# Where the transposes stand among the expert products of a mixture of experts

## The chip, the cores and the metric

The kernel runs on one core of one Trainium2 chip. The metric is the device time in microseconds (us) of one execution. TensorE is called PE here, its weight loads PEld, VectorE DVE, ScalarE ACT, GpSimd POOL; SyncE (SP) only issues DMAs.

## The reference

The reference is a two-layer encoder on 1024 tokens of width 1024, all in float32. Layer 0 mixes tokens by RWKV-7, layer 1 by a gated linear recurrence (HGRN2). Behind each mixer comes a mixture of experts: 32 experts with 512 inner columns, of which each token uses two. The change touches only this mixture, cut here to its core:

```python
def moe_ffn(u, w_rg, b_rg, w_re, b_re, w_in, w_out):
    # top-1 group of 4, then top-2 of its 8 experts: expert, gate
    ...
    def expert_block(args):
        xb, e = args                      # up to 128 rows of one expert
        hgu = xb @ w_in[e]                # 1024 -> 2 * 512
        return (jax.nn.silu(hgu[:, :MOE_FF]) * hgu[:, MOE_FF:]) @ w_out[e]   # 512 -> 1024
    yp = lax.map(expert_block, (xp.reshape(nblk, MOE_BLK, D), block_e)).reshape(P, D)
    return jnp.zeros_like(u).at[tok_s].add(yp[dest] * g_s[:, None].astype(u.dtype))
```

## The kernel before

Both layers run a mixer, a routing stage and then `mixture` (L2045), which calls `experts` (L1756), a loop for overfull experts (`extra_experts`, L1892) and the weighted sum (`combine`, L2007). Barriers of all engines stand between the stages.

`experts` runs 24 steps, written out in full. The routing has ranked the experts. A **full step** handles one expert with up to 128 rows; a **half step** handles two experts with up to 64 rows each. There are 16 full and 8 half steps; `STEP_ORDER` (L1620) places the half steps at steps 3, 6, 9, 12, 14, 17, 19 and 22, so steps 0 to 2 and 23 are full.

In a step, PE works on these things:

- **x transposes** (`turn_x`, L1732): the gathered rows `e.x` (128 rows by 1024) are transposed in 8 blocks of 128x128 into PSUM banks 2 and 3. DVE then multiplies them by the norm's gain into `e.x_t` (`x_t`, L1854).
- **the up-product**, in two calls of `product` (L1816): "low" takes the first four blocks of `e.x_t`, "high" the last four. Each has 4 blocks by 2 column halves, so 8 products in a full step, each 128x128 by 128x512. In a half step each of the 8 places holds two products, one for each expert, with 64 stationary columns each; they write to the upper and the lower 64 rows of the same bank. One product of float32 leaves two matmul records; two products of a half step start within 0.01 us of each other.
- **activation transposes** (`turn_act`, L1737): ACT takes silu of the one half of the up-product (L1881), DVE multiplies by the other (L1865), and PE transposes the result in 4 blocks into bank 4; ACT copies it into `e.act_t` (L1889).
- **the down-product** ("out"): 4 blocks by 2 column halves, 8 places again, into banks 6 and 7; ACT and DVE each copy one half out (L1886, L1872), and POOL scatters the rows to memory.

PE's order is written by hand (L1830 to L1848). For step n it is: low(n), high(n), the 8 x transposes of n+1, the down-product of step n-1, the 4 activation transposes of n. So the down-product lies one step behind, and its work covers silu, the product on DVE and the gain. Step 0 has no down-product to run; after step 23 only the last one is left.

The weights come through a ring of 8 units of 2 MB (four blocks of an expert). A full step uses 3 units, a half step 6. SP issues the load of unit n when unit n-8 has been used (L1787): the last product on a unit raises the semaphore `used`. POOL gathers the rows of step n+2 when those of step n have been transposed (L1800), and scatters those of step n-1 when both copies are done.

Of the kernel before, what the change touches and what calls it, by code (L numbers as in the profile page):

```python
# [28 lines left out]
P = 128  # L29
T = 1024  # L30
D = 1024
KT = D // P
TT = T // P
HALF = 512
NH = T // HALF
# [14 lines left out]
FF = 512  # L50
# [6 lines left out]
STEPS = WHOLE + (EXPERTS - WHOLE) // 2  # L57
# [28 lines left out]
def spread(ap, axis, n):  # L86

    shape = list(ap.shape)
    shape.insert(axis, n)
    return ap.unsqueeze(axis).to_broadcast(shape)  # L90


class Stage:


    used, taken = set(), set()
# [1618 lines left out]
class ExpertBuffers:  # L1715
# [13 lines left out]
        self.out_p = self.psum[:, 6:8, :].rearrange("p a e -> p (a e)")  # L1729


    def turn_x(self, t, c, b):  # L1732
        for k in range(KT):
            mm = t.transpose(self.x_p[:, k, :], self.x[b][:, k * P:(k + 1) * P], c.ident[:])
        return mm

    def turn_act(self, t, c):  # L1737
        for k in range(FF // P):
            mm = t.transpose(self.act_p[:, k, :], self.act[:, k * P:(k + 1) * P], c.ident[:])
        return mm  # L1740


def gather(g, d, x, rows, bound):

    return g.indirect_dma_start(out=x, out_offset=None, in_=d.rows,
                                in_offset=bass.IndirectOffsetOnAxis(ap=rows, axis=0),
                                bounds_check=bound, oob_is_err=False)


def scatter(g, d, out, rows, bound):  # L1750
    return g.indirect_dma_start(out=d.expert_rows, in_=out, in_offset=None,  # L1751
                                out_offset=bass.IndirectOffsetOnAxis(ap=rows, axis=0),
                                bounds_check=bound, oob_is_err=False)


def experts(nc, c, d, r, weights, layer, name):  # L1756

    with Stage(nc, name) as s:
        e = ExpertBuffers(s, r)
        gathered = [d.pool_dma[layer][f"gathered{b}"] for b in range(2)]
        scattered = [d.pool_dma[layer][f"scattered{b}"] for b in range(2)]
        used, x_turned, x_ready, act_ready, act_turned = (
            s.sem(x) for x in ("used", "x_turned", "x_ready", "act_ready", "act_turned"))
        silu_ready, act_t_ready, out_low, out_high, finished = (
            s.sem(x) for x in ("silu_ready", "act_t_ready", "out_low", "out_high", "finished"))
        block = s.block()
        numbers = {(u.part, u.step, u.half): n for n, u in enumerate(UNITS)}  # L1770

        def unit_numbers(part, step):
            return [numbers[part, step, q] for q in (None, 0, 1) if (part, step, q) in numbers]

        def used_up(part, step):

            return max(unit_numbers(part, step)) + 1

        def rows_of(table, step):
            return table[:, STEP_ORDER[step]:STEP_ORDER[step] + 1]  # L1780

        @block.sync
        def _(sp):
            expert = {}
            for n in range(RING, len(UNITS)):
                u = UNITS[n]
                sp.wait_ge(used, n - RING + 1)  # L1787
                if u.place < FIXED:
                    weights.load(sp, n, u.place)
                    continue  # L1790
                if u.part == "low":
                    expert[u.place] = sp.value_load(r.order[0:1, u.place:u.place + 1], min_val=0, max_val=EXPERTS - 1)
                weights.load(sp, n, expert[u.place])

        @block.gpsimd
        def _(g):
            last_token, last_assignment = g.to_reg(T - 1), g.to_reg(2 * T - 1)
            for n in range(STEPS + 1):
                if n + 2 < STEPS:
                    g.wait_ge(x_turned, n + 1)  # L1800
                    gather(g, d, e.x[n % 2], rows_of(r.gather_row, n + 2), last_token).then_inc(gathered[n % 2], 16)
                if n:
                    g.wait_ge(out_low, n)
                    g.wait_ge(out_high, n)
                    scatter(g, d, e.out[(n - 1) % 2][:], rows_of(r.scatter_row, n - 1), last_assignment
                            ).then_inc(scattered[(n - 1) % 2], 16)
            for b in range(2):
                g.wait_ge(scattered[b], 16 * (STEPS // 2))

        @block.tensor  # L1810
        def _(t):
            def turn_x(n):
                t.wait_ge(gathered[n % 2], 16 * (n // 2) + 16)
                e.turn_x(t, c, n % 2).then_inc(x_turned, 1)

            def product(part, n, bank, left, k0):  # L1816
                mine = unit_numbers(part, n)
                for m in mine:
                    t.wait_ge(weights.arrived[m % RING], 16 * (m // RING) + 16)
                for k in range(KT // 2):  # L1820
                    for a in range(NH):
                        for m in mine:
                            rows = slice(0, P) if UNITS[m].half is None else slice(UNITS[m].half * HEAD, (UNITS[m].half + 1) * HEAD)
                            mm = t.matmul(e.psum[rows, bank + a, :], left[:, k0 + k, rows],  # L1824
                                          weights.units[m % RING][:, k, a * HALF:(a + 1) * HALF],
                                          start=(part != "high" and k == 0), stop=(part != "low" and k == KT // 2 - 1))
                            if k == KT // 2 - 1 and a == NH - 1:
                                mm.then_inc(used, 1)

            turn_x(0)  # L1830
            for n in range(STEPS + 1):
                if n < STEPS:
                    t.wait_ge(x_ready, n + 1)
                    if n:
                        t.wait_ge(act_ready, n)
                    product("low", n, 0, e.x_t, 0)
                    product("high", n, 0, e.x_t, KT // 2)
                if n + 1 < STEPS:
                    turn_x(n + 1)
                if n:  # L1840
                    t.wait_ge(act_t_ready, n)
                    if n >= 2:
                        t.wait_ge(out_low, n - 1)
                        t.wait_ge(out_high, n - 1)
                    product("out", n - 1, 6, e.act_t, 0)
                if n < STEPS:
                    t.wait_ge(act_ready, n + 1)
                    e.turn_act(t, c).then_inc(act_turned, 1)  # L1848

        @block.vector  # L1850
        def _(v):
            gain = spread(c.gain(1, layer), 2, P)

            def x_t(n):  # L1854
                v.wait_ge(x_turned, n + 1)
                v.tensor_tensor(e.x_t[:], e.x_p, gain, ALU.mult).then_inc(x_ready, 1)

            x_t(0)
            r.finish(v, finished)
            for n in range(STEPS + 1):  # L1860
                if n < STEPS:
                    v.wait_ge(silu_ready, n + 1)
                    if n:
                        v.wait_ge(act_turned, n)
                    v.tensor_mul(e.act[:], e.silu[:], e.value_p).then_inc(act_ready, 1)  # L1865
                if n + 1 < STEPS:
                    x_t(n + 1)
                if n:
                    v.wait_ge(used, used_up("out", n - 1))
                    if n >= 3:  # L1870
                        v.wait_ge(scattered[(n - 1) % 2], 16 * ((n - 1) // 2))
                    v.tensor_copy(e.out[(n - 1) % 2][:, HALF:D], e.out_p[:, HALF:D]).then_inc(out_high, 1)  # L1872

        @block.scalar
        def _(a):
            for n in range(STEPS + 1):
                if n < STEPS:
                    a.wait_ge(used, used_up("high", n))
                    if n:
                        a.wait_ge(act_ready, n)  # L1880
                    a.activation(e.silu[:], e.gate_p, ACT.Silu).then_inc(silu_ready, 1)  # L1881
                if n:
                    a.wait_ge(used, used_up("out", n - 1))
                    if n >= 3:
                        a.wait_ge(scattered[(n - 1) % 2], 16 * ((n - 1) // 2))
                    a.activation(e.out[(n - 1) % 2][:, 0:HALF], e.out_p[:, 0:HALF], ACT.Copy).then_inc(out_low, 1)  # L1886
                if n < STEPS:
                    a.wait_ge(act_turned, n + 1)
                    a.activation(e.act_t[:], e.act_p, ACT.Copy).then_inc(act_t_ready, 1)  # L1889


# [695 lines left out]
```

## Time and profile before

| | us |
|---|---|
| median of 3 runs | 3145.62 (3142.65 to 3147.25) |
| the profiled execution's own time | 3144.24 |
| its span | 3142.4 |
| PE busy | 2675.7, 85% of the span |
| DVE, ACT, POOL busy | 892.4, 533.8, 262.6 |
| weights for the expert steps, in queue q1 of layer 0 | 184.56 MB |

In a row of a timeline the first number is the start in us from the start of the span, the second the length of the merged group, then engine, line, operation, output<-input, the active rows*columns of the array, the moved shape, and xcount records. In brackets stands how long the engine was idle before, and what released it. The end of a matmul is modelled, so a group's length runs past the start of the next; the distance between two starts is what counts. A row of windows gives start:end, length, then for PE, PEld, DVE, ACT and POOL the busy us (xinstructions), then the granted PE clock as a share of 2.4 GHz, the DMA engines' busy share and GB/s.

### The profile page before, as it was taken

The page shows a single profiled execution, that of the slowest core. Times are in us where ns is not written, and L with a number is a line of the kernel's source. Part 1 is how long each engine was busy: PE and PEld are TensorE (multiplying, and loading weights), DVE is VectorE, ACT ScalarE, POOL GpSimd, SP SyncE. Part 2 cuts the span into 40 slices and gives each one's busy share as a digit, 9 for nine tenths or more (in the row PEclk, how much of TensorE's full clock was granted, in tenths as well). Part 3 has the DMA queues.
Part 4 walks back from the last instruction along what each step waited for, and adds up shares of the span by engine and source line. Part 5 has one row for each costly group of instructions (what it writes and reads, how often), then busy time and mean ns, then how long its engine had stood idle before and what let it go on. Part 6 is the DMA issues. An engine that isn't in the chain of part 4 may idle for free. (4 is left out here: it accounts for less than half of the span.)

```text
span 3142.4 us, 44471 instructions
## 1 busy us (share of the span) xinstructions
PE 2675.7 (85%) x18608; PEld 1444.7 (46%) x18608; DVE 892.4 (28%) x1589; ACT 533.8 (17%) x832; POOL 262.6 (8%) x233
## 2 busy tenths in 40 slices
PE   5798996888787795999999759998667959999993
PEld 2343443788785253444444234443653534444441
DVE  6332002556555434111111130001763331111112
ACT  3342001232233311000000032000222100000000
POOL 0000001011111400001010000000111011010100
PEclk9998998999999897999999879999788979999997
DMA  3242222212314613899999542211324059999995
GB/s 116 106 146 95 73 94 81 80 43 50 76 47 162 230 80 133 325 412 409 413 405 398 230 165 99 80 40 61 83 97 156 34 202 354 415 416 414 411 400 228
DMA packets 264766, 617.50 MB, mean 197 GB/s; under 512 B 37377, under 2 KB 128658, under 8 KB 262546
## 3 DMA queue, kind: packets, MB, share of 16 engines
q1 hardware_dynamic: 233362, 524.72, 44.8%
q10 hardware_dynamic: 17408, 56.63, 4.6%
q0 software_dynamic: 13824, 33.58, 2.7%
q8 instruction: 142, 2.33, 0.3%
q14 instruction: 30, 0.25, 0.0%
HBM read 545.67 MB, written 85.98 MB: 201 GB/s over the span
## 5 line engine op out<-in xcount | busy, mean ns | idle before, releaser
L1824 PE MATMUL moe_first_psum<-moe_ring,moe_first_x_t 128*64 128x512 f32 (+1 forms) x1504 | 509.1, 599 | 7.6 <-DMA moe_ring<-in_moe_w_in 4.0
L560 PE MATMUL proj_psum<-proj_mix,proj_ring 128*128 128x512 f32 x768 | 337.7, 600 | 15.8 <-ACTq L72 10.1
L1824 PEld LDWEIGHTS moe_first_psum<-moe_ring,moe_first_x_t 128*64 128x64 f32 (+1 forms) x1504 | 198.3, 165 | 280.5 <-issue 275.6
L1824 PE MATMUL moe_first_psum<-moe_ring,moe_first_act_t 128*128 128x512 f32 (+1 forms) x800 | 282.1, 594 | 0.0
L1422 PE MATMUL moe_route_psum<-moe_ring,trunk_mixed 128*128 128x512 f32 x512 | 230.8, 606 | 23.1 <-PEq L106 23.1
L560 PEld LDWEIGHTS proj_psum<-proj_mix,proj_ring 128*128 128x128 f32 x768 | 147.2, 193 | 200.9 <-issue 189.2
L1865 DVE TENSOR_TENSOR moe_first_act<-moe_first_silu,moe_first_psum 128x512 f32<-128x512 f32 x48 | 33.0, 688 | 689.2 <-ACT moe_first_silu L1881 689.2
L2108 PE MATMUL hproj_psum<-trunk_mixed,hproj_ring 128*128 128x512 f32 x512 | 222.4, 597 | 7.1 <-DMA hproj_ring<-in_hg_in 7.1
L1824 PE MATMUL moe_first_psum<-trunk_mixed,moe_first_x_t 128*128 128x512 f32 (+1 forms) x544 | 196.1, 593 | 0.0
L1824 PEld LDWEIGHTS moe_first_psum<-moe_ring,moe_first_act_t 128*128 128x128 f32 (+1 forms) x800 | 105.8, 162 | 131.5 <-issue 131.5
L1422 PEld LDWEIGHTS moe_route_psum<-moe_ring,trunk_mixed 128*128 128x128 f32 x512 | 97.0, 194 | 137.8 <-issue 137.8
L2108 PEld LDWEIGHTS hproj_psum<-trunk_mixed,hproj_ring 128*128 128x128 f32 x512 | 98.1, 192 | 130.7 <-issue 123.4
L1003 PE MATMUL scan_psum<-scan_xp,scan_x 64*64 64x128 f32 (+1 forms) x2560 | 150.0, 258 | 0.0
L1881 ACT ACTIVATE moe_first_silu<-moe_first_psum 128x512 f32<-128x512 f32 x48 | 28.7, 599 | 649.8 <-PE moe_first_psum L1824 649.8
L1751 POOL DMA_INDIRECT expert_rows<-moe_first_out,moe_scatter_row x48 | 48.2, 1005 | 942.9 <-DVE moe_first_out L1872 918.8
L1003 PEld LDWEIGHTS scan_psum<-scan_xp,scan_x 64*64 64x64 f32 x2560 | 126.3, 140 | 0.0
L1824 PEld LDWEIGHTS moe_first_psum<-trunk_mixed,moe_first_x_t 128*128 128x128 f32 (+1 forms) x544 | 76.4, 165 | 101.8 <-issue 101.8
L1003 PE MATMUL scan_psum<-scan_x,scan_xp 64*64 64x64 f32 x2048 | 89.9, 228 | 30.7 <-ACT scan_x L979 29.7
L2124 PE MATMUL hproj_psum<-hproj_wide,trunk_mixed 128*128 128x512 f32 x256 | 110.0, 592 | 0.0
L1872 DVE COPY moe_first_out<-moe_first_psum 128x512 f32<-128x512 f32 x48 | 33.2, 692 | 264.0 <-PE moe_first_psum L1824 264.0
L1824 PE MATMUL moe_first_psum<-trunk_mixed,moe_first_act_t 128*128 128x512 f32 (+1 forms) x224 | 98.9, 594 | 1.4 <-ACT moe_first_act_t L1889 1.4
L1003 PEld LDWEIGHTS scan_psum<-scan_x,scan_xp 64*64 64x64 f32 x2048 | 83.7, 144 | 32.6 <-ACT scan_x L979 31.4
(338 smaller groups left out, 3076.6 us busy)
## 6 DMA issues: line engine op xcount, KB each, us to landing
moe_ring<-in_moe_w_in SPq DMA_DIRECT2D x94, 2048.0 KB, 18.1
moe_ring<-in_moe_w_out SPq DMA_DIRECT2D x50, 2048.0 KB, 20.1
trunk_mixed<-in_moe_w_in SPq DMA_DIRECT2D x34, 2048.0 KB, 20.6
trunk_mixed<-in_moe_w_out SPq DMA_DIRECT2D x14, 2048.0 KB, 21.5
moe_ring<-expert_rows SPq DMA_DIRECT2D x16, 1024.0 KB, 8.4
proj_ring<-in_rw_in SPq DMA_DIRECT2D x12, 1024.0 KB, 6.1
moe_ring<-gate_cm SPq DMA_DIRECT2D x16, 512.0 KB, 4.4
normed_rows<-moe_x SPq DMA_DIRECT2D x16, 512.0 KB, 2.6
```

The lines of the kernel that those rows point to most:

```text
L560: mm = pe.matmul(psum[:, bank + half, :], ring[slot][:, k, part * P:(part + 1) * P], src[:, k, half * HALF:(half + 1) * HALF], start=(k == ...
L1003: mm = t.matmul(out[to[h], m - pairs.start, :], lhs[source[h], m, :], rhs[source[h], m, :], start=True, stop=True)
L1422: mm = t.matmul(psum[:, 2 * (i % 2) + a, :], u[:, k, i * P:(i + 1) * P], w_out[:, k, a * HALF:(a + 1) * HALF], start=(k == 0), stop=(k == ...
L1751: return g.indirect_dma_start(out=d.expert_rows, in_=out, in_offset=None, out_offset=bass.IndirectOffsetOnAxis(ap=rows, axis=0), bounds_ch ...
L1824: mm = t.matmul(e.psum[rows, bank + a, :], left[:, k0 + k, rows], weights.units[m % RING][:, k, a * HALF:(a + 1) * HALF], start=(part != " ...
L1865: v.tensor_mul(e.act[:], e.silu[:], e.value_p).then_inc(act_ready, 1)
L1872: v.tensor_copy(e.out[(n - 1) % 2][:, HALF:D], e.out_p[:, HALF:D]).then_inc(out_high, 1)
L1881: a.activation(e.silu[:], e.gate_p, ACT.Silu).then_inc(silu_ready, 1)
L2108: mm = t.matmul(psum[:, 2 * (n % 2) + half, :], ring[n // 2][:, k, (n % 2) * P:(n % 2 + 1) * P], u[:, k, half * HALF:(half + 1) * HALF], s ...
L2124: mm = t.matmul(psum[:, 4 + 2 * (i % 2) + a, :], u[:, k, i * P:(i + 1) * P], wide[a][:, k, :], start=(k == 0), stop=(k == KT - 1))
```

## The change

Two new helpers make one transpose each. `product` takes two more arguments. With `x_of` it puts one x transpose behind each of its 8 places; with `act_of` it puts one activation transpose behind each of its last 4 places. The x transposes of step n+1 now stand in high(n), the activation transposes of step n in the down-product of step n-1. Step 0 keeps its activation transposes as a block, since it has no down-product. Waits go with the first transpose of a set, the semaphore with the last. The last x transpose stands behind the last product of high(n), as the last activation transpose does behind the last of the down-product.

DVE's gain and ACT's copy now wait for two things each: that the transposes are done, and that the product that reads the old contents of their target is done.

```diff
+    def turn_x_part(self, t, c, b, k):
+        return t.transpose(self.x_p[:, k, :], self.x[b][:, k * P:(k + 1) * P], c.ident[:])
+    def turn_act_part(self, t, c, k):
+        return t.transpose(self.act_p[:, k, :], self.act[:, k * P:(k + 1) * P], c.ident[:])
...
+            def part_of_x(n, k):
+                if k == 0:
+                    t.wait_ge(gathered[n % 2], 16 * (n // 2) + 16)
+                mm = e.turn_x_part(t, c, n % 2, k)
+                if k == KT - 1:
+                    mm.then_inc(x_turned, 1)
+            def part_of_act(n, k):
+                if k == 0:
+                    t.wait_ge(act_ready, n + 1)
+                mm = e.turn_act_part(t, c, k)
+                if k == FF // P - 1:
+                    mm.then_inc(act_turned, 1)
...
-            def product(part, n, bank, left, k0):
+            def product(part, n, bank, left, k0, x_of=None, act_of=None):
...
+                        at = k * NH + a
+                        if x_of is not None:
+                            part_of_x(x_of, at)
+                        if act_of is not None and at >= KT - FF // P:
+                            part_of_act(act_of, at - (KT - FF // P))
...
-                    product("high", n, 0, e.x_t, KT // 2)
-                if n + 1 < STEPS:
-                    turn_x(n + 1)
+                    product("high", n, 0, e.x_t, KT // 2, x_of=n + 1 if n + 1 < STEPS else None)
...
-                    product("out", n - 1, 6, e.act_t, 0)
-                if n < STEPS:
+                    product("out", n - 1, 6, e.act_t, 0, act_of=n if n < STEPS else None)
+                elif n < STEPS:
                     t.wait_ge(act_ready, n + 1)
                     e.turn_act(t, c).then_inc(act_turned, 1)
...
                 v.wait_ge(x_turned, n + 1)
+                if n:
+                    v.wait_ge(used, used_up("high", n - 1))
...
                     a.wait_ge(act_turned, n + 1)
+                    if n:
+                        a.wait_ge(used, used_up("out", n - 1))
```

## Rows read from the trace of the kernel before

**Rows 1.** The page, span in 40 slices: granted TensorE clock, DMA busy.
```profile
PEclk9998998999999897999999879999788979999997
DMA  3242222212314613899999542211324059999995
```

**Rows 2.** Windows, the expert steps of both layers: stretch, length, engines busy, clock, DMA, GB/s.
```profile
1246.40:1786.90 540.50, 534.84 (x1816) 229.63 (x1816) 61.29 (x81) 40.69 (x72) 44.49 (x44) 0.99 0.94 371
2560.20:3095.80 535.60, 533.38 (x1816) 229.56 (x1816) 61.00 (x80) 40.44 (x71) 44.49 (x44) 1.00 0.94 375
```

**Rows 3.** Timeline, PE, two up-products with DMA waits: start, length, what [idle before].
```profile
1663.40 7.09 PE L1824 MATMUL moe_first_psum<-moe_ring,moe_first_x_t 128*64 128x512 f32 x32
1674.07 8.70 PE L1824 MATMUL moe_first_psum<-moe_ring,moe_first_x_t 128*64 128x512 f32 x32 [3.58 <-DMA moe_ring<-in_moe_w_in]
1682.71 1.09 PE L1734 MATMUL moe_first_psum<-ident,moe_x 128*128 128x128 f32 x8
...
3043.69 7.09 PE L1824 MATMUL moe_first_psum<-trunk_mixed,moe_first_x_t 128*64 128x512 f32 x32
3058.24 1.09 PE L1734 MATMUL moe_first_psum<-ident,moe_x 128*128 128x128 f32 x8
```

**Rows 4.** Timeline, PE, a full step and a half step of layer 0.
```profile
1426.72 7.03 PE L1824 MATMUL moe_first_psum<-trunk_mixed,moe_first_x_t 128*128 128x512 f32 x16
1433.59 1.04 PE L1734 MATMUL moe_first_psum<-ident,moe_x 128*128 128x128 f32 x8
1434.46 7.03 PE L1824 MATMUL moe_first_psum<-trunk_mixed,moe_first_act_t 128*128 128x512 f32 x16
1441.33 0.60 PE L1739 MATMUL moe_first_psum<-ident,moe_first_act 128*128 128x128 f32 x4
1441.86 13.95 PE L1824 MATMUL moe_first_psum<-moe_ring,moe_first_x_t 128*64 128x512 f32 x64
1455.74 1.09 PE L1734 MATMUL moe_first_psum<-ident,moe_x 128*128 128x128 f32 x8
1456.67 7.03 PE L1824 MATMUL moe_first_psum<-moe_ring,moe_first_act_t 128*128 128x512 f32 x16
```

**Rows 5.** Timeline, PEld, the loads of the first transposes of two groups.
```profile
1433.16 0.14 PEld L1734 LDWEIGHTS moe_first_psum<-ident,moe_x 128*128 128x128 f32 x1 [0.24 <-issue]
...
1455.74 0.86 PEld L1734 LDWEIGHTS moe_first_psum<-ident,moe_x 128*128 128x128 f32 x8 [0.81 <-issue]
```

**Rows 6.** Timeline, PE, full up-product followed by a half down-product.
```profile
1757.28 13.90 PE L1824 MATMUL moe_first_psum<-moe_ring,moe_first_x_t 128*128 128x512 f32 x32
1771.11 0.64 PE L1824 MATMUL moe_first_psum<-moe_ring,moe_first_act_t 128*64 128x512 f32 x1
```

**Rows 7.** Timeline, end of step 0 of layer 0, all engines.
```profile
1262.36 1.04 PE L1734 MATMUL moe_first_psum<-ident,moe_x 128*128 128x128 f32 x8
1262.56 0.60 ACT L1881 ACTIVATE moe_first_silu<-moe_first_psum 128x512 f32<-128x512 f32 x1 [18.17 <-PE moe_first_psum L1824]
...
1263.87 1.22 DVE L1856 TENSOR_TENSOR moe_first_x_t<-moe_first_psum,norm_cols 128x1024 f32<-128x1024 f32 x1
1265.15 0.70 PE L1824 MATMUL moe_first_psum<-moe_ring,moe_first_x_t 128*128 128x512 f32 x1 [0.48 <-DVE moe_first_x_t L1856]
```

**Rows 8.** Timeline, PE, last transposes and last product of layer 0.
```profile
1778.13 0.66 PE L1739 MATMUL moe_first_psum<-ident,moe_first_act 128*128 128x128 f32 x4
1779.47 7.13 PE L1824 MATMUL moe_first_psum<-trunk_mixed,moe_first_act_t 128*128 128x512 f32 x16 [0.69 <-ACT moe_first_act_t L1889]
```

**Rows 9.** Timeline, POOL, one gather; and the DMA view's row of gathers, us to landing.
```profile
1400.19 1.02 POOL L1745 DMA_INDIRECT moe_x<-normed_rows,moe_gather_row  x1 [0.31 <-issue]
...
moe_x<-normed_rows,moe_gather_row POOLq DMA_INDIRECT x22, 8.7
```

**Rows 10.** Windows, two stretches that bear on the clock.
```profile
1674.00:1678.00 4.00, 3.93 (x12) 1.40 (x14) 0.00 (x0) 0.00 (x0) 0.00 (x0) 0.58 1.11 413
100.00:124.00 24.00, 12.00 (x50) 4.13 (x48) 12.00 (x11) 15.59 (x14) 0.00 (x0) 1.00 0.48 175
```

More of the change, by code:

```diff
@@ L1729, in __init__ @@
         self.out_p = self.psum[:, 6:8, :].rearrange("p a e -> p (a e)")
+    def turn_x_part(self, t, c, b, k):
+        return t.transpose(self.x_p[:, k, :], self.x[b][:, k * P:(k + 1) * P], c.ident[:])
+    def turn_act_part(self, t, c, k):
+        return t.transpose(self.act_p[:, k, :], self.act[:, k * P:(k + 1) * P], c.ident[:])
     def turn_x(self, t, c, b):
         for k in range(KT):
-            mm = t.transpose(self.x_p[:, k, :], self.x[b][:, k * P:(k + 1) * P], c.ident[:])
+            mm = self.turn_x_part(t, c, b, k)
         return mm
@@ L1738, in turn_act @@
         for k in range(FF // P):
-            mm = t.transpose(self.act_p[:, k, :], self.act[:, k * P:(k + 1) * P], c.ident[:])
+            mm = self.turn_act_part(t, c, k)
         return mm
```

## The prediction

> **What bounds the kernel now.** I read the page's slices first. The expert steps are the two stretches with DMA at 8 or 9, slices 17 to 22 and 34 to 39; PE's clock there is 9 throughout [rows 1]. The windows over exactly these steps show PE busy for 534.84 of 540.50 us in layer 0 and 533.38 of 535.60 us in layer 1, at a clock of 0.99 and 1.00, with DMA at 0.94 of its time [rows 2]. So PE sets the time, and DMA is close behind it. DVE, at 61 us, and ACT, at 41 us, are far from any bound [rows 2]; what counts of them is only whether they are late at one place.
>
> How close DMA is shows in the timeline of PE. Once in layer 0 PE waits 3.58 us for a weight unit in the middle of a half step's up-product [rows 3]. That product takes 1682.71 - 1663.40 = 19.31 us. An undisturbed one takes 1455.74 - 1441.86 = 13.88 us [rows 4]. The loss is 5.43 us: the wait, and 5.43 - 3.58 = 1.85 us of slow products behind it, for the 4 us right after the wait have a clock of 0.58, most of them at the lower level of 1.2 GHz [rows 10]. Layer 1 loses 3058.24 - 3043.69 - 13.88 = 0.67 us at such a place [rows 3]. Everything else in the steps is PE's own pace.
>
> That pace is what the change alters, so I worked it out from starts. A full step's low or high product: 1433.59 - 1426.72 = 6.87 us for 16 records, 0.429 us each. Eight x transposes behind a full product: 0.87 us, 0.109 us each. Four activation transposes and then a half product: 0.53 us, where 4 x 0.109 = 0.44 is due: 0.09 over. The half up-product: 13.88 us, where 2 x 6.87 = 13.74 is due: 0.14 over. Eight x transposes behind the half product: 0.93 us, 0.06 over 0.87 [rows 4]. So one excursion between half-width products and full-width transposes costs 0.09 + 0.14 + 0.06 = 0.29 to 0.30 us beyond the array time. Around full products the same excursion costs nothing that two decimals show. These rows are one of 16 half steps, and the others repeat their distances. I use 0.30.
>
> The load rows say why. Before a transpose behind a full product, PEld starts at 1433.16, a whole record ahead of the transpose at 1433.59. Behind a half product it starts at 1455.74, together with its transpose: nothing was loaded ahead, and the array had run empty [rows 5, 4].
>
> The Trainium skill, "TensorEngine Tiling (Array Packing)", section Key Properties, states that changing the tiling mode drains TensorE, while changing tiles within one mode does not. This trace agrees, with the 0.30 us above. It is a rule that speaks against this change; the sum below would be the same without it.
>
> **The change part by part.**
>
> *Array work.* Nothing is removed: 8 + 4 transposes of 0.109 us per step stay, only elsewhere. PE runs its products in order, so a transpose among them adds the same 0.109 us that it added behind them. Gain: 0.
>
> *Excursions in half steps.* This is the main term. Before, a half step's up-product has one group of transposes before it and one behind it, and so has its down-product: one excursion each. After, in high(n) of a half step, each of the 8 x transposes stands alone between half products; the last is followed by the down-product, as before. That makes 7 excursions more. In a half step's down-product 3 of the 4 activation transposes have half products on both sides: 3 more. All 8 half steps have both (steps 3 to 22, each with a next step). So 8 x 10 = 80 per layer, 160 in all, x 0.30 = **48.0 us**. No row shows a lone transpose between half products, so I bound it. From below: where a half product follows a full product without a transpose between, it starts at 1771.11, 13.83 us behind the start of 32 full records, where 32 x 0.429 = 13.74 are due: 0.09 [rows 6]. If leaving half width were free and only coming back cost this, the term is 160 x 0.09 = 14 us. From above: nothing overlaps the drain, the load and the refill on either side, and a little is lost to the order of the two halves; I allow 0.35, 56 us. A gain is excluded here, since each transpose keeps its own 0.109 us. I take 0.30: in the measured excursion the first transpose already bears the load that was not made ahead, and the last bears the way back, and a lone one is both.
>
> *Excursions in full steps.* 15 full steps with 7, and 15 with 3 inner transposes: 150 per layer, 300 in all. Rows 4 show less than 0.01 us at a change from product to transpose and back. Between 0 and 3 us; I take 1.
>
> *Step 0.* It has no down-product to cover the gain. PE's last product of high(0) gives way to the first transpose at 1262.36, ACT starts silu at 1262.56, DVE ends the gain at 1265.09 (1263.87 + 1.22), and low(1) starts at 1265.15 [rows 7]. That chain hangs on the last product of high(0), which now comes behind 7 transposes: 7 x 0.109 = 0.76 us later, and so all of it. Before, the 8 transposes lay in the shadow of this chain. 2 x 0.76 = **1.5 us**. DVE's added wait has long been met.
>
> *Last step.* Before, the 4 activation transposes of step 23 ran in the shadow of ACT, which first copies the output half: 1778.13 to 1779.47 is 1.34 us, of which the page gives 0.69 as a wait for ACT [rows 8]. Now three of them come before the last product of step 22, whose end starts ACT: 3 x 0.109 = 0.33 us per layer, 0.7 in all. ACT's added wait is for that same product, which its copy has waited for already.
>
> *Gathers and activations needed earlier.* The first x transpose now comes some 6 us earlier, inside high(n). The gather of step n+2 is issued at 1400.19, and its rows were transposed at 1433.59, two groups later; gathers land 8.7 us after issue [rows 9, 4]. Some 18 us of slack are left: cost 0, and if the cover were gone, PE with all products behind it would wait that difference in each step. The activation is needed after 5 of 8 places of the down-product, 10 records x 0.429 = 4.3 us after its start; silu, DVE's product and their waits need about 1.5 us after the high product (in rows 7 the gain starts at 1263.87, with the activation before it). Cost 0. Transposes still in the queue hold up nothing on SP or POOL except the release of units, which shifts by under 1 us of a ring 8 deep.
>
> *The DMA waits.* When PE needs about 3 us more per half step (10 x 0.30), the lead that DMA lost by 1670 us, after six half steps, is no longer lost: by then PE is 18 us later, and the wait was 3.58. Both waits go, with the slow clock behind the first: 5.43 + 0.67 = **-6.1 us**. What is late next is PE itself.
>
> *Sum.* 48.0 + 1 + 1.5 + 0.7 - 6.1 = 45.1 us on the profiled execution's 3144.24 (its span of 3142.4 and 1.8 around it, which does not change): 3189.3. The median of the runs is 1.4 us above that execution, so it would give 3190.7; that difference may well be the waits that go. I say 3190.
>
> **The rivals.**
>
> *A lone transpose pays no drain* (it is loaded ahead between the two halves, or the second product hides it). For it: no row shows one alone. Against: every group behind a half product pays, to within 0.01 us. Then 1 + 1.5 + 0.7 remain, and the DMA waits stay: +3, 3148. This is the case that the change costs nothing.
>
> *It pays half*: only the way back, or only the way out. 160 x 0.15 = 24, + 3.2 - 6.1 = +21: 3166.
>
> *The strewn transposes hide behind the products.* PE would save 12 x 0.109 = 1.31 us per step. This is the other sign. Against: transposes start 0.429 behind a product's record and the next one 0.109 behind them, with nothing overlapping [rows 4]. It would also meet DMA: its wait at 1670 stands in step 19, so what PE saves before comes back as waiting, and only the four steps behind count, with the one or two behind the place in layer 1: 6 x 1.31 = 8 us at most. It decides only from where a transpose costs less than 0.109 us. 3137.
>
> *The clock falls in the half steps.* There PE would have a drain of about 0.3 us in each 1.27 us. After the idle time of 3.58 us the clock stood at 0.58 of its full level [rows 3, 10], so idle can bring it down. Against: between 100 and 124 us PE was busy for only 12.00 of 24.00 us at a clock of 1.00, that is 2.4 GHz [rows 10]; a half step's products with their drains stay busy for over 70%. If every half step lost the 1.85 us that the wait's slow products lost, that is 16 x 1.85 = 30 more: 3220.
>
> **How the numbers follow.** Forecast 78%; no drain 6%; half 7%; hidden 3%; slow clock 3%; others, such as a late gather, 3%. The forecast's own range is 3181 (0.25 per excursion) to 3198 (0.35). The range reaches to the half case: 3167 to 3200. A measurement of this kernel can tell about 0.2% from no change, 6.3 us. Faster by more: 4%; within: 7%; slower by more: 89%.
>
> **What would show it.** In the changed trace a half step's high product with its 8 transposes spans about 6.9 + 8 x (0.109 + 0.30), 10.2 us, and a full one's 6.87 + 0.87, 7.7 us. Each load of a transpose behind a half product starts with it, not ahead. The waits for moe_ring from DMA are gone, DMA's share in the steps falls from 0.94 to about 0.90, the clock stays at 1.00, and PE's busy time changes little while idle put down to issue grows. Wrong it would be if the half products keep 0.429 us per record around a lone transpose, if a full step grows, or if PE waits for a gather or for the activation.

## The result, and the profile after

The changed kernel takes 3194.20 us in the median of 4 runs (3193.74 to 3200.97), the kernel before 3146.43 us in the same comparison (3142.65 to 3153.36). The ratio is 1.0154, with a 95% interval of 1.0132 to 1.0177: slower by 48 us. Forecast were 3190 us and a range of 3167 to 3200.

From the page of the changed kernel, clock and DMA in 40 slices:

```profile
PEclk8998998999898897999999879998788979999997
DMA  3242222312114604999999442202224159999994
```

The span of this execution is 3199.3 us, 56.9 us more than before. Not all of that is the change's. The windows over the expert steps of both layers, from the first product to the last (columns as in [rows 2]), say what is:

```profile
1259.10:1819.80 560.70, 557.59 (x1816) 217.24 (x1816) 61.25 (x81) 40.13 (x72) 44.64 (x44) 1.00 0.91 358
2594.20:3154.40 560.20, 557.35 (x1816) 217.20 (x1816) 61.02 (x80) 39.91 (x71) 44.62 (x44) 1.00 0.91 359
```

The steps take 560.70 and 560.20 us, where they took 540.50 and 535.60 [rows 2]: 20.2 + 24.6 = 44.8 us. The sum forecast 45.1. The clock is at 1.00 in both, and DMA's share fell from 0.94 to 0.91. PE's busy time grew as much as the steps did, from 534.84 to 557.59 us in layer 0: the end of a matmul is modelled, and the view counts as busy what is lost between starts. So what follows is read from starts. The other 12 us of this execution lie in stages that the change does not touch, most of them in the scan of layer 0, told at the end.

PE's waits in layer 0's steps (who waited, for whom, us in total, times, the longest):

```profile
PE moe_first_psum L1733 <- PEq L106: 9.2, 1, 9.2
PE moe_first_psum L1846 <- DVE moe_first_x_t L1883: 1.8, 2, 1.3
PE moe_first_psum L1736 <- DVE moe_first_act L1892: 1.4, 1, 1.4
PE moe_first_psum L1846 <- ACT moe_first_act_t L1918: 1.0, 1, 1.0
```

No row names moe_ring from DMA. Layer 1's view has the same four groups: the waits of [rows 3] are gone in both layers. What is left are the start of the stage, step 0 and the last step.

The timeline of PE through a half step's up-product, with the x transposes strewn into its second half, and on to the down-product:

```profile
1461.60 7.95 PE L1846 MATMUL moe_first_psum<-moe_ring,moe_first_x_t 128*64 128x512 f32 x36
1469.48 0.33 PE L1733 MATMUL moe_first_psum<-ident,moe_x 128*128 128x128 f32 x1
1469.74 1.08 PE L1846 MATMUL moe_first_psum<-moe_ring,moe_first_x_t 128*64 128x512 f32 x4
1470.75 0.33 PE L1733 MATMUL moe_first_psum<-ident,moe_x 128*128 128x128 f32 x1
1471.01 1.08 PE L1846 MATMUL moe_first_psum<-moe_ring,moe_first_x_t 128*64 128x512 f32 x4
...
1477.36 1.08 PE L1846 MATMUL moe_first_psum<-moe_ring,moe_first_x_t 128*64 128x512 f32 x4
1478.37 0.33 PE L1733 MATMUL moe_first_psum<-ident,moe_x 128*128 128x128 f32 x1
1478.54 4.46 PE L1846 MATMUL moe_first_psum<-moe_ring,moe_first_act_t 128*128 128x512 f32 x10
```

Each of the 8 places now takes 1470.75 - 1469.48 = 1.27 us. Of that 0.858 is the product (two records of 0.429 for each of the two experts, side by side) and 0.109 the transpose; 0.30 is neither. The transpose starts 1.01 us behind the first half product, where 0.86 is due, and the half product starts 0.26 us behind the transpose, where 0.11 is due: half of the loss lies on either side of the lone transpose. The whole up-product with them takes 1478.54 - 1461.60 = 16.94 us. Before it was 1456.67 - 1441.86 = 14.81 [rows 4]: 2.13 more, or 7 x 0.30.

The records of one place stand singly at the end of layer 0's last half down-product (of each pair one record is shown):

```profile
1809.84 0.33 PE L1736 MATMUL moe_first_psum<-ident,moe_first_act 128*128 128x128 f32 x1
1810.11 0.64 PE L1846 MATMUL moe_first_psum<-moe_ring,moe_first_act_t 128*64 128x512 f32 x1
1810.59 0.59 PE L1846 MATMUL moe_first_psum<-moe_ring,moe_first_act_t 128*64 128x512 f32 x1
1811.12 0.33 PE L1736 MATMUL moe_first_psum<-ident,moe_first_act 128*128 128x128 f32 x1
```

From the transpose to the product it is 0.27 us (0.11 due), from the product's first record to its second 0.48 (0.43 due), and from that to the next transpose 0.53 (0.43 due).

The same in a down-product of full width:

```profile
1482.83 0.27 PE L1736 MATMUL moe_first_psum<-ident,moe_first_act 128*128 128x128 f32 x1
1482.94 1.02 PE L1846 MATMUL moe_first_psum<-moe_ring,moe_first_act_t 128*128 128x512 f32 x2
1483.80 0.27 PE L1736 MATMUL moe_first_psum<-ident,moe_first_act 128*128 128x128 f32 x1
```

Here a place takes 0.97 us, 0.858 + 0.109: nothing is lost that two decimals show. The loads show the difference once more. Two rows of PEld in the half product, and one in the full one:

```profile
1470.75 0.14 PEld L1733 LDWEIGHTS moe_first_psum<-ident,moe_x 128*128 128x128 f32 x1 [0.81 <-issue]
1471.01 0.20 PEld L1846 LDWEIGHTS moe_first_psum<-moe_ring,moe_first_x_t 128*64 128x64 f32 x4
...
1483.37 0.14 PEld L1736 LDWEIGHTS moe_first_psum<-ident,moe_first_act 128*128 128x128 f32 x1 [0.24 <-issue]
```

The transpose at 1483.80 in the full product has its load at 1483.37, a record ahead. The one at 1470.75 has it at 1470.75, and the half products' loads at 1471.01 start with the product too. On either side of the lone transpose nothing is loaded ahead.

### The profile page after: what moved, and what is told of

Read it like the earlier page. It is cut to its first block and busy times, and to the rows that moved or that the text cites. A ratio compares the mean times of both kernels' runs of the same rounds, so it can differ in the third digit from the quotient of the medians.

```text
span 3199.3 us, 44563 instructions
## 1 busy us (share of the span) xinstructions
PE 2731.9 (85%) x18608; PEld 1430.7 (45%) x18608; DVE 893.6 (28%) x1589; ACT 533.4 (17%) x832; POOL 263.1 (8%) x233
## 5 line engine op out<-in xcount | busy, mean ns | idle before, releaser
L1846 PE MATMUL moe_first_psum<-moe_ring,moe_first_x_t 128*64 128x512 f32 (+1 forms) x1504 | 539.4, 602 | 3.6 <-DVE moe_first_x_t L1883 3.6
L1846 PE MATMUL moe_first_psum<-moe_ring,moe_first_act_t 128*128 128x512 f32 (+1 forms) x800 | 300.6, 599 | 0.0
L1846 PEld LDWEIGHTS moe_first_psum<-moe_ring,moe_first_x_t 128*64 128x64 f32 (+1 forms) x1504 | 180.7, 164 | 226.5 <-issue 212.7
L1846 PE MATMUL moe_first_psum<-trunk_mixed,moe_first_x_t 128*128 128x512 f32 (+1 forms) x544 | 214.6, 600 | 0.0
L1846 PEld LDWEIGHTS moe_first_psum<-moe_ring,moe_first_act_t 128*128 128x128 f32 (+1 forms) x800 | 96.8, 163 | 107.7 <-issue 103.4
L1733 PEld LDWEIGHTS moe_first_psum<-ident,moe_x 128*128 128x128 f32 x384 | 54.9, 144 | 179.0 <-issue 179.0
L1733 PE MATMUL moe_first_psum<-ident,moe_x 128*128 128x128 f32 x384 | 111.5, 298 | 17.5 <-PEq L106 17.5
```

The source lines that it names most:

```text
L1733: return t.transpose(self.x_p[:, k, :], self.x[b][:, k * P:(k + 1) * P], c.ident[:])
```

## The experiments

Each kernel was compared with the kernel before, run beside it on the same chip. The chip and the time of the kernel before differ from one comparison to another. Under "steps" stands how much longer than in the kernel before the two layers' expert steps are in the profiled executions, one of each kernel, from the first transpose to the start of the last product (542.9 + 538.3 = 1081.1 us before). It is the better measure, since the scan's length drifts by several us from run to run. Places in a product are counted from 0 to 7. The ratio comes from all runs of both kernels and is not the quotient of the medians.

| kernel | median us | kernel before | ratio (95%) | steps |
|---|---|---|---|---|
| the change | 3194.20 | 3146.43 | 1.0154 (1.0132 to 1.0177) | +44.7 |
| full_only | 3146.11 | 3143.67 | 1.0013 (1.0000 to 1.0026) | -0.8 |
| half_only | 3190.42 | 3143.67 | 1.0167 (1.0145 to 1.0189) | +42.1 |
| pairs | 3157.86 | 3143.67 | 1.0063 (1.0041 to 1.0085) | +15.3 |
| narrow | 3163.57 | 3143.67 | 1.0068 (1.0045 to 1.0090) | +17.2 |
| x_only2 | 3176.27 | 3147.61 | 1.0102 (1.0082 to 1.0122) | +29.0 |
| act_only2 | 3154.81 | 3147.61 | 1.0029 (1.0015 to 1.0043) | +8.6 |
| reorder2 | 3147.61 | 3147.61 | 1.0010 (0.9998 to 1.0022) | -1.4 |

### Strewn in full steps alone (full_only), in half steps alone (half_only)

The edit replaces the places of the transposes in `product`; the second kernel has the two lists the other way round.

```diff
+                        half = len(mine) > 1
                         if x_of is not None:
-                            part_of_x(x_of, at)
+                            for j in ([[]] * 7 + [list(range(8))] if half else [[j] for j in range(8)])[at]:
+                                part_of_x(x_of, j)
...
```

> The transposes are strewn in the full steps' products alone; in the 16 half-step up- and down-products of both layers they stand as a block behind the product. Theory (the cost is the excursion between half-width products and full-width transposes, 0.30 us each): no inner excursion is left, only step 0's 1.5 us and under 1 us of the rest, and PE again meets the DMA waits: about 3148, within 3 us of the kernel before (3146). Rival (strewing costs by itself, wherever it stands: a lone transpose breaks the run of loads): 15 of 23 steps are strewn, so some 60% of the 48 us stays, 3175. In the trace the theory wants 0.43 us before and 0.11 us behind each lone transpose in full products.

> The transposes are strewn in the half steps' products alone, and stand as blocks in the full steps. Theory: all 160 excursions are there, 48 us, and the DMA waits of about 6 us are gone, step 0 is as before: 3146 + 48 + 0.7 - 6 = 3189, some 2 us under the changed kernel at most 5. Rival (strewing costs everywhere): 8 of 23 steps, 3163.

Measured: the first kernel is 1.0013 of the kernel before, the second 1.0167, as much as the whole change. The steps of the first are 0.8 us shorter than before: 1.5 us of step 0 are added, its DMA waits are shorter (2.7 us in layer 0 and 0.3 in layer 1, where they were 3.6 and 0.4), and the clock stays at 1.00 behind them, where the kernel before lost 1.85 us more in layer 0. Strewing costs next to nothing where the widths agree. The second kernel's steps are 2.6 us shorter than the change's, which is step 0's 1.5 and about 1 for the full steps. The timeline of PE in full_only, a half up-product's end with its block of eight, then a strewn full down-product:

```profile
1454.61 4.03 PE L1846 MATMUL moe_first_psum<-moe_ring,moe_first_x_t 128*64 128x512 f32 x18
1458.57 1.09 PE L1733 MATMUL moe_first_psum<-ident,moe_x 128*128 128x128 f32 x8
1459.50 4.46 PE L1846 MATMUL moe_first_psum<-moe_ring,moe_first_act_t 128*128 128x512 f32 x10
1463.79 0.27 PE L1736 MATMUL moe_first_psum<-ident,moe_first_act 128*128 128x128 f32 x1
1463.90 1.02 PE L1846 MATMUL moe_first_psum<-moe_ring,moe_first_act_t 128*128 128x512 f32 x2
1464.76 0.27 PE L1736 MATMUL moe_first_psum<-ident,moe_first_act 128*128 128x128 f32 x1
```

The block behind the half product takes 0.93 us as before, and the places of the down-product 1464.76 - 1463.79 = 0.97. Over seven places of a full up-product in the same trace, 1474.54 to 1481.33, it is 6.79 us where 7 x 0.967 = 6.77 are due: some 0.003 us a place. The rival, that strewing costs wherever it stands, is out.

### Two by two (pairs)

```diff
+                            for j in ([[], [0, 1], [], [2, 3], [], [4, 5], [], [6, 7]] if half else [[j] for j in range(8)])[at]:
+                                part_of_x(x_of, j)
...
+                            for j in ([[]] * 5 + [[0, 1], [], [2, 3]] if half else [[]] * 4 + [[j] for j in range(4)])[at]:
+                                part_of_act(act_of, j)
```

> In half steps the transposes stand two by two: x transposes behind places 1, 3, 5 and 7, those of the activations behind places 5 and 7. Full steps as in the changed kernel. The number of transposes is the same; the inner excursions fall from 10 to 4 in a half step. Theory (the price is per change of width, not per transpose): 96 excursions fewer, 96 x 0.30 = 29 us less than the changed kernel, 3165. Rival (each transpose behind a half product loses its load's head start, so the price is per transpose): no change, 3194. In between, if the price of 0.30 is partly per transpose: each 0.05 us per transpose moves the time by about 5.

Measured: +15.3 us of steps against the change's +44.7: 29.4 less, where 96 x 0.30 = 29 were expected. The forecast of 3165 was 7 too high as an absolute time: it stood on the changed kernel's median from another comparison. The kernel before was 2.8 us faster in this one (3143.67 against 3146.43); where the other 4 come from no run shows, and they do not lie in the steps.

The timeline of PE in pairs, a half up-product:

```profile
1455.10 1.94 PE L1846 MATMUL moe_first_psum<-moe_ring,moe_first_x_t 128*64 128x512 f32 x8
1456.97 0.44 PE L1733 MATMUL moe_first_psum<-ident,moe_x 128*128 128x128 f32 x2
1457.34 1.94 PE L1846 MATMUL moe_first_psum<-moe_ring,moe_first_x_t 128*64 128x512 f32 x8
1459.21 0.44 PE L1733 MATMUL moe_first_psum<-ident,moe_x 128*128 128x128 f32 x2
```

Two places and two transposes take 1459.21 - 1456.97 = 2.24 us: 2 x 0.858 + 2 x 0.109 = 1.93, and 0.30 once. The price is per change of width and back, not per transpose.

### Transposes of the same width as the half products (narrow)

```diff
...
+        for q in range(2):
+            mm = t.matmul(self.x_p[q * HEAD:(q + 1) * HEAD, k, :],
+                          self.x[b][:, k * P + q * HEAD:k * P + (q + 1) * HEAD], c.ident[:], start=True, stop=True)
...
```

> In half steps each strewn transpose is made as two products with the identity, with 64 stationary columns each, that write the upper and lower 64 rows: the same width as the half products around them. A float32 product runs in two passes where a transpose needs one, so each costs about 0.214 us (a quarter of the 0.858 us of a place) instead of 0.109. Theory (the change of width is what costs): the 160 excursions go, 192 such transposes cost 0.105 more each, 20 us: 3194 - 48 + 20 = 3166, and in the trace half products follow at 0.43 without a gap. Rival (it is the change of stationary operand from one tile to another, or of output bank, that costs, whatever the width): 3194 + 20 = 3214.

Measured: +17.2 us of steps, 27.5 less than the change; 48 - 20 = 28 were expected. The timeline at a half step:

```profile
1318.73 7.95 PE L1856 MATMUL moe_first_psum<-moe_ring,moe_first_x_t 128*64 128x512 f32 x36
1326.51 0.39 PE L1736 MATMUL moe_first_psum<-ident,moe_x 128*64 128x128 f32 x4
1326.72 1.03 PE L1856 MATMUL moe_first_psum<-moe_ring,moe_first_x_t 128*64 128x512 f32 x4
1327.58 0.39 PE L1736 MATMUL moe_first_psum<-ident,moe_x 128*64 128x128 f32 x4
1327.80 1.03 PE L1856 MATMUL moe_first_psum<-moe_ring,moe_first_x_t 128*64 128x512 f32 x4
```

A strewn transpose, now 64 columns wide and in two passes, takes 0.21 to 0.22 us, and the half products around it follow at once: a place takes 1327.58 - 1326.51 = 1.07 us, 0.858 + 0.214, with nothing left over. Operand, identity and output bank change as often as in the changed kernel, so that rival is out. Two things differ from the changed kernel: the width no longer changes, and the transposes have become ordinary products. The second is not what counts. Where a full product follows the last of these narrow ones, the width changes without a transpose of the old kind, and the full product still starts late:

```profile
1334.04 0.39 PE L1736 MATMUL moe_first_psum<-ident,moe_x 128*64 128x128 f32 x4
1334.36 4.56 PE L1856 MATMUL moe_first_psum<-moe_ring,moe_first_act_t 128*128 128x512 f32 x10
```

That is 0.32 us where 0.214 are due, as the half product behind a full one was 0.09 late in the kernel before [rows 6]; and among full products transposes cost next to nothing (full_only). So it is the change of width that costs. The Trainium skill, "TensorEngine Tiling (Array Packing)", section Key Properties, says the same in general: a change of mode drains TensorE, a change of tile within a mode does not; the runs put 0.30 us and 0 beside it.

### One part alone (x_only2, act_only2)

The other set stands as a block behind place 7, in full and half steps alike.

```diff
-                        if act_of is not None and at >= KT - FF // P:
-                            part_of_act(act_of, at - (KT - FF // P))
+                        if act_of is not None:
+                            for j in ([[]] * 7 + [list(range(4))])[at]:
+                                part_of_act(act_of, j)
```

> Only the x transposes are strewn; those of the activations stand as a block behind the down-product. Theory: 7 inner excursions in each of 16 half up-products, 112 x 0.30 = 34 us, step 0's 1.5 and under 1 for the full steps, less the DMA waits of 6: 29 above the kernel before, 3173. Rival (a place's price depends on what waits there, the gathers for x, the activation for the others): the one part holds all 48 us and the other none, 3190 or 3147.

> Only the activation transposes are strewn. Theory: 3 inner excursions in each of 16 half down-products, 48 x 0.30 = 14 us, and 0.7 at the last step; the steps are 0.9 us longer per half step, 5.4 us by the place of the DMA wait, more than its 3.6, so most of the 6 us of waits go: 9 to 12 above the kernel before, 3154. Together with the run that strews x alone the excess over the kernel before, waits put back, has to come to that of the change: 34 + 14 = 48. Rival as there.

Measured: +29.0 and +8.6 us of steps. With the 6.1 us of DMA waits put back to each, and step 0's 1.5 us taken off the first and the last step's 0.5 off the second, that is 33.6 and 14.2: 112 and 48 excursions at 0.30 us each, if the full steps' share of under 1 us is left in. Neither part holds all of it, so the rival is out. No DMA wait is left in either.

### The kernel before with half steps later (reorder2)

```diff
-    rest = [next(halves) if x == "2" else next(whole) for x in "211211211212112121121"]
+    rest = [next(halves) if x == "2" else next(whole) for x in "211211211211211212121"]
```

> The kernel before, with two of the half steps one step later (half steps at 3, 6, 9, 12, 15, 18, 20 and 22 instead of 3, 6, 9, 12, 14, 17, 19 and 22). Nothing is strewn. Theory (the DMA waits of the kernel before come when half steps, with 12 MB of weights each in 22 us, have used up the lead of the ring): the lead lasts longer, the waits shrink or go, up to 6 us less, 3138 to 3142. Rival (the wait is a disturbance of DMA that has nothing to do with the lead): the same time as before. If it only moves to step 22, less than 2 us are gained.

Measured: 1.0010 (0.9998 to 1.0022), no gain. The edit moves three half steps, not two as the text above says (14 to 15, 17 to 18, 19 to 20). The wait of layer 0 is still there, in the half step at 22; in the kernel before it stood at 19:

```profile
1738.56 7.09 PE L1824 MATMUL moe_first_psum<-trunk_mixed,moe_first_x_t 128*64 128x512 f32 x32
1748.79 7.09 PE L1824 MATMUL moe_first_psum<-moe_ring,moe_first_x_t 128*64 128x512 f32 x32 [3.14 <-DMA moe_ring<-in_moe_w_in]
1755.81 1.09 PE L1734 MATMUL moe_first_psum<-ident,moe_x 128*128 128x128 f32 x8
```

That was the third case of what was expected. It does not show that the wait follows the half steps' places: in full_only, whose order is that of the kernel before, layer 0's wait stands in step 22 too:

```profile
1742.56 7.09 PE L1846 MATMUL moe_first_psum<-moe_ring,moe_first_x_t 128*64 128x512 f32 x32 [2.70 <-DMA moe_ring<-in_moe_w_in]
```

Layer 1's wait stands in step 22 in all three kernels. The waits of reorder2 (3.1 and 1.4 us) are no shorter than those of the kernel before (3.6 and 0.4). Its steps are 1.4 us shorter all the same, since the clock is at 1.00 behind its wait in layer 0, where it was at 0.58 in the kernel before [rows 10]: 0.5 us more of waits, 1.85 less of slow products. No version better than both was found.

## Why the prediction was right

*What bounds.* PE set the time, before and after; its own pace changed and nothing else took over. One sign of the prediction did not come: PE's busy time was to change little and idle time put down to issue to grow, but busy time took up the whole loss (534.84 to 557.59 us). The signs that stand on starts came. The high product with its 8 transposes spans 10.01 us in the trace; the 10.2 forecast counted an eighth excursion in full, though behind its transpose comes the full-width down-product, as before.

*Excursions in half steps.* Forecast 160 x 0.30 = 48.0. The lone transpose between half products, which no row before showed, costs 0.30 us in each place of the timeline above. That the price is the change of width is shown by two runs: the same transposes two by two save 29 us, and the same number at the products' width save 48 less the 20 of their second pass. The lower bound of 0.09 was low for what it stood for: coming back costs that and 0.05 more between the product's two records, and leaving half width costs 0.10 (0.53 instead of 0.43 to the transpose) and the 0.06 of the load that was not made ahead. So either way alone is about half of the 0.30.

*Excursions in full steps.* Forecast 1 us, between 0 and 3. At the 0.003 us a place of full_only, 300 of them make 0.9.

*Step 0.* Forecast 0.76 us per layer. Timeline of the end of step 0, all engines:

```profile
1275.92 0.27 PE L1733 MATMUL moe_first_psum<-ident,moe_x 128*128 128x128 f32 x1
1276.12 0.60 ACT L1908 ACTIVATE moe_first_silu<-moe_first_psum 128x512 f32<-128x512 f32 x1 [18.99 <-PE moe_first_psum L1846]
...
1277.43 1.22 DVE L1883 TENSOR_TENSOR moe_first_x_t<-moe_first_psum,norm_cols 128x1024 f32<-128x1024 f32 x1
...
1278.70 1.13 PE L1846 MATMUL moe_first_psum<-moe_ring,moe_first_x_t 128*128 128x512 f32 x2 [0.48 <-DVE moe_first_x_t L1883]
```

The last x transpose now starts at 1275.92, and low(1) at 1278.70. From the start of silu to low(1) it is 2.58 us, as 1265.15 - 1262.56 = 2.59 before [rows 7]. From the first product of the stage (1259.13) to silu it is 16.99 us, before 1262.56 - 1246.41 = 16.15: 0.84 later, where 7 transposes make 0.76; I did not follow the other 0.08. The chain itself did not change, it starts later.

*Last step.* Forecast 0.33 us per layer. PE at the last transpose and the last product of layer 0:

```profile
1811.12 0.33 PE L1736 MATMUL moe_first_psum<-ident,moe_first_act 128*128 128x128 f32 x1
1812.39 2.84 PE L1846 MATMUL moe_first_psum<-trunk_mixed,moe_first_act_t 128*128 128x512 f32 x6 [0.95 <-ACT moe_first_act_t L1918]
```

From the last transpose to the last product it is 1.27 us now, with 0.95 put down to ACT; before it was 1.34 from the first of four, with 0.69 [rows 8]. Three transposes were in ACT's shadow and are so no longer: 3 x 0.109 = 0.33 us come ahead of it, and what is left behind is 0.07 shorter, so 0.26 per layer.

*Gathers and activations needed earlier.* Forecast 0. Neither appears among PE's waits, apart from step 0.

*The DMA waits.* Forecast -6.1 us. They are gone in both layers of all six kernels whose half steps became longer, and stayed in both layers of full_only and reorder2, whose half steps did not. So the term was right for the profiled execution that it was added to. A part of its size was chance: the 1.85 us of slow products behind the wait stand in the kernel before alone, while the waits of 2.7 and 3.1 us in full_only and reorder2 have a clock of 1.00 behind them. That the wait comes because half steps use up the lead of the ring is likely but not shown: three of them one step later did not shorten it (reorder2).

*Sum.* 44.8 measured in the steps against 45.1: the sum was right term by term, within 0.5 us each. The medians differ by 47.8; the 3 us beyond lie within the drift of the stages that the change leaves alone.

*The rivals.* No drain, half of it, and transposes hidden behind products are all out by the 1.27 us of a place. The slow clock is out by 1.00 in both windows, though by the starts 0.30 of each 1.27 us are neither product nor transpose there.

## What to carry to other kernels

Count how often an order of work switches TensorE between products of 64 and of 128 stationary columns, and price each way out and back from a place where the trace shows one (0.30 us here); in these runs spreading small operations among large ones was nearly free only where the widths agreed. Work that is strewn among products on the same engine was not hidden by them (a full-width place takes 0.97 us, 0.858 + 0.109): it only moves, and it gains something only if it stood where somebody waited. And where a block ran in the shadow of another engine's chain (step 0, the last step), moving it ahead of that chain makes it cost what it takes.

## What was not expected

The stages that the change leaves alone are not equally long in two executions. The scan of layer 0, windows over the same instructions (columns as in [rows 2]), first in the kernel before:

```profile
534.50:983.70 449.20, 384.78 (x11264) 369.45 (x11264) 259.77 (x556) 129.95 (x294) 55.32 (x37) 0.96 0.21 52
```

and in the changed kernel:

```profile
537.30:996.50 459.20, 392.71 (x11265) 377.05 (x11265) 260.00 (x556) 130.51 (x294) 55.47 (x37) 0.94 0.21 51
```

The same 11264 or 11265 records take 449.20 and 459.20 us, at clocks of 0.96 and 0.94. PE is busy for 85% of the stretch there, and how often the clock falls to 1.2 GHz differs from run to run. In the nine profiled executions of this study the scan's products span, from first to last start, 447 us in four, where the clock was at 1.2 GHz for 30 to 41 us of it, and 452 to 457 us in the other five, where it was so for 49 to 57. Why the clock falls more often in some was not looked into. The kernel before itself ran in 3135 to 3155 us, which this drift would account for in part. So the length of the changed stage tells a change of a few us better than the median of the whole.
